# Attention scores from rounded halves of queries and keys, and one program block for the gate table and the experts

## The reference, cut to what matters

```
scores = einsum("brqhd,brkwhd->bhrqkw", q, k_g) * (dh ** -0.5) + bias   # local, 8 heads of 64, window 8 x 16
sc = einsum("bqngd,bknd->bngqk", qblk, k) * scale                       # group: 8 query heads, 2 key heads
sc = einsum("thpc,hpnc->thpn", q, sub_keys); top_s, top_i = top_k(sc, 16)
act = einsum("cd,ced->ce", xc, u[ic]); hid = gelu(act) * gc             # 128 experts per token
out = einsum("ce,ced->cd", hid, v[ic])
```

## Time and profile before

| what | value |
|---|---|
| median of 3 runs | 2273.9 us (2271.93 to 2278.22) |
| the profiled execution, its own time | 2281.19 us |
| its span, first to last instruction | 2278.3 us |
| busy: PE, DVE, ACT, POOL | 2155.6, 1501.3, 824.6, 671.5 us |
| mean granted TensorE clock | 0.973 of 2.4 GHz |
| phase_attend | about 128 to 244 us of the span |
| last product of phase_table, first of phase_experts | 1014.4 and 1027.4 us |

### The profile page before, as it was taken

How to read it: one execution, slowest core, us unless ns; L and a number is a source line. 1 busy time by engine, 2 the same in 40 slices (tenths; PEclk the granted TensorE clock), 3 DMA queues, 4 the chain that set the end, 5 groups by cost and what they waited for, 6 DMA issues and landing times. The chain is left out here.

```text
span 2278.3 us, 28638 instructions
## 1 busy us (share of the span) xinstructions
PE 2155.6 (95%) x10851; PEld 1863.2 (82%) x10851; DVE 1501.3 (66%) x2670; ACT 824.6 (36%) x1319; POOL 671.5 (29%) x440
## 2 busy tenths in 40 slices
PE   7999999999999999979999999999998999988899
PEld 6777788788999999979787877899986798876667
DVE  4645434425987889855889879869997534447644
ACT  3345423322333347733333333333334332222312
POOL 0100000000278877511434435436651000014200
PEclk9999999999999999999999999999998999988999
DMA  5321533301677878888999999979993222210320
GB/s 214 117 88 47 203 148 111 126 32 58 168 174 201 217 196 216 254 279 294 386 388 383 386 384 374 388 266 374 372 327 117 105 93 93 93 56 1 115 98 37
DMA packets 220232, 454.52 MB, mean 199 GB/s; under 512 B 32320, under 2 KB 137792, under 8 KB 213440
## 3 DMA queue, kind: packets, MB, share of 16 engines
q1 hardware_dynamic: 164800, 318.39, 40.9%
q0 software_dynamic: 55296, 134.31, 17.8%
HBM read 406.17 MB, written 46.47 MB: 199 GB/s over the span
## 5 line engine op out<-in xcount | busy, mean ns | idle before, releaser
L984 PE MATMUL bank<-XH,H 128*128 128x384 f32 x1024 | 349.8, 342 | 22.3 <-PEq L1229 12.6
L986 PE MATMUL bank<-XH,L 128*128 128x384 f32 x1024 | 345.8, 338 | 0.0
L985 PE MATMUL bank<-XL,H 128*128 128x384 f32 x1024 | 345.7, 338 | 0.0
L1734 PE MATMUL bank<-Vh,Hh 128*128 128x512 f32 x768 | 302.3, 394 | 17.0 <-DVE Hl L1829 17.0
L1735 PE MATMUL bank<-Vl,Hh 128*128 128x512 f32 x768 | 301.6, 393 | 0.0
L1736 PE MATMUL bank<-Vh,Hl 128*128 128x512 f32 x768 | 301.3, 392 | 0.0
L1065 POOL DMA_INDIRECT gates<-rows_sb x128 | 245.7, 1920 | 116.6 <-DVE rows_sb L1467 61.3
L1770 ACT ACTIVATE Vh<-Vr 128x1024 fp32r<-128x1024 f32 x128 | 135.8, 1061 | 293.4 <-PE bank L1736 151.8
L1021 POOL DMA_INDIRECT ring<-in_v,kq x128 | 186.3, 1456 | 177.5 <-DVE x_res L1033 76.3
L984 PEld LDWEIGHTS bank<-XH,H 128*128 128x128 f32 x1024 | 195.2, 191 | 26.0 <-issue 15.0
L985 PEld LDWEIGHTS bank<-XL,H 128*128 128x128 f32 x1024 | 195.0, 190 | 1.1
(11 more groups left out here) (393 smaller groups left out, 4398.3 us busy)
## 6 DMA issues: line engine op xcount, KB each, us to landing
Vr<-in_v SPq DMA_DIRECT2D x128, 512.0 KB
ur<-in_u SPq DMA_DIRECT2D x86, 512.0 KB
W<-in_w_stream SPq DMA_DIRECT2D x19, 2048.0 KB, 8.0
Gr<-gates SPq DMA_DIRECT2D x32, 768.0 KB
XT<-in_u SPq DMA_DIRECT2D x42, 512.0 KB
early<-ar SPq DMA_DIRECT2D x92, 192.0 KB
A<-early SPq DMA_DIRECT2D x92, 192.0 KB
XT<-in_w_mixer SPq DMA_DIRECT2D x14, 1024.0 KB
```

The costliest lines, as they stand in the source:

```text
L984: pe.matmul(ps, h[:, k], c.Xh[:, k, 0:DN], start=k == 0, stop=False)
L985: pe.matmul(ps, h[:, k], c.Xl[:, k, 0:DN], start=False, stop=False)
L986: mm = pe.matmul(ps, l[:, k], c.Xh[:, k, 0:DN], start=False, stop=k == KT - 1)
L1734: pe.matmul(ps, Hh[r][:, tok], Vh[r][:, cut], start=p == 0, stop=False)
```

## The change

Three things are changed together. (1) Scores: local attention uses halves of queries and keys, three fp32r products of 64 rows each (head h lies on partitions 0 to 63 or 64 to 127, with no padding). Group attention writes each query twice, on both halves of the partitions, and stacks the key's high half on its own 64 partitions and the low half on the other 64: one product of 128 rows gives hi x (hi + lo), a second one of 64 rows lo x hi. (2) The halves are made in phase_project: each group head is turned by PE, rounded by ACT and subtracted by DVE, in three portions of 4, 4 and 2 heads behind three pieces of projection; the memsets of `qz` go. Half of the storage is a slot of the weight ring, so one load of 2 MB (block 6) moves from phase_project to the end of phase_attend. (3) phase_table and phase_experts share one block. Loads of v and gates are written between the last eight turns of the table, the 14 dots are spread over the nine last conversions, six dots of the experts stand in the six lead blocks, PE waits for the table's copies before it reuses their banks.

```
@@ phase_project @@
+        def local_hi(act, g):
+            to, scale = (a.kh, 1.0) if g < 16 else (a.qh, DH ** -0.5)
+            act.activation(col_rows(to[:, g % 4]), by_col(bank(g)[:]), ACT.Copy, scale=scale).then_inc(grp_a, 1)
...
+        def turned_lo(dve, h):
+            dve.wait_ge(rout, h + 1)
+            if h < HEADS:
+                cut = own(h // 4)
+                dve.scalar_tensor_tensor(out=a.qgl[cut, h % 4], in0=c.bank[h % 4][cut, :], scalar=DH ** -0.5, in1=a.qgh[cut, h].bitcast(F32),
+                                         op0=ALU.mult, op1=ALU.subtract).then_inc(rout_d, 1)
...
+                if b != B_KA:
+                    c.load_w(sp, b + RING)
...
-            pool.memset(a.qz[:], 0.0).then_inc(set0, 1)
...
+                dve.tensor_tensor(a.q_rows[:, tt], twice(S1, ATT_W), twice(S2, ATT_W), ALU.add)
...
+                if 0 <= i - TURN < len(TURNED):
+                    for h in range(4 * (i - TURN), 4 * (i - TURN) + TURNED[i - TURN]):
@@ phase_attend @@
+            sp.wait_ge(scored, UNITS)
+            c.load_w(sp, B_KA + RING)
...
                     if h < HEADS:
-                        qT, kT = a.qz[:, h], a.kT[:, h // 2, KEY0[q]:KEY0[q] + KEYS]
+                        pe.matmul(ps, a.qh[cut, n, tok], a.kh[cut, n, keys], start=True, stop=False)
+                        pe.matmul(ps, a.qh[cut, n, tok], a.kl[cut, n, keys], start=False, stop=False)
+                        mm = pe.matmul(ps, a.ql[cut, n, tok], a.kh[cut, n, keys], start=False, stop=True)
                     else:
-                        qT, kT = a.qzb[:, h - HEADS], a.kTb[:]
-                    pe.matmul(psS[i % 3][:, 0:width(i)], qT[:, q * P:(q + 1) * P], kT, start=True, stop=True).then_inc(scored, 1)
+                        pe.matmul(ps, a.qgh[:, h - HEADS, tok], a.kg[:, n], start=True, stop=False)
+                        mm = pe.matmul(ps, a.qgl[cut, g, tok], a.kg[cut, n], start=False, stop=True)
+                    mm.then_inc(scored, 1)
@@ phase_table, phase_experts @@
-            turns(EL, E_LAST)
...
+            pe.wait_ge(copied, 2 * (DT - SCATTERED) * NSL)
...
-            fill(DOTS_TABLE, EARLY + 2)
+            los = count["lo"]
+            for n in range(los, EARLY + 2):
+                fill(DOTS_TABLE - D_LAST + D_LAST * (n + 1 - los) // (EARLY + 2 - los), n + 1)
...
-        block = ctx.enter_context(nc.Block())
...
+            for i in range(E_LAST):
+                early.turn(sp, EARLY - E_LAST + i)
+                if i == FREE:
+                    early.table_done(sp)
+                if FREE <= i < FREE + RR:
+                    load_v(i - FREE)
+                elif i == FREE + RR:
+                    sca.done(sp)
+                    load_g(0)
             for m in range(LEAD):
                 load_u(m + 3)
-                if m < RR:
-                    load_v(m)
...
             for q in range(LEAD):
                 lo_u(q + 2)
+                gat.dot(dve, DOTS_TABLE + q)
@@ build @@
+                block = joint.enter_context(nc.Block())
```

More of the change, by code:

```diff
@@ L194, in shared @@
         top = self.nc.sbuf_base
+        self.kq_at = top - (LOW + 4 * KT * P) * 4
         self.H, self.L = ([self.nc.alloc_sbuf_tensor_at(f"{n}{i}", [P, KT * P], F32R, offset=top - (at - i) * KT * P * 4)[:] for i in range(2)]
@@ L401, in out @@
             def out(b):
-                for g in range(4 * b, 4 * b + 4, 2 if b in (B_QB, B_KVB, B_QA) else 1):
+                for g in range(4 * b, 4 * b + 4, 2 if b in (B_QB, B_KVB) else 1):
                     act.wait_ge(grp, g + 1)
[L404 to L408, removed]
+                    if g < 12:
+                        project_out(g, copy, grp_a)
+                    else:
+                        if g == 12:
+                            act.wait_ge(roped, 1)
+                        if g == 16:
+                            act.wait_ge(rturn, HEADS + KV_HEADS)
+                        local_hi(act, g)
             for tt in range(0, TT, 2):
@@ L422, in _ @@
                     out(ends[i - 3])
[L423 to L428, removed]
+                if 0 <= i - TURN - 3 < len(TURNED):
+                    at = i - TURN - 3
+                    for h in range(4 * at, 4 * at + TURNED[at]):
+                        turned_hi(act, h)
             out(B_QA)
@@ L506, in _ @@
             link(last)
-            dve.wait_ge(set0, 2)
             for tt in range(TT):
[L509 to L514, removed]
+                twice = lambda x, w: x[:, tt, 0:w].rearrange("p (h w) -> p h w", w=DH).unsqueeze(2).broadcast_to([P, w // DH, 2, DH])
+                dve.tensor_tensor(a.q_rows[:, tt], twice(S1, ATT_W), twice(S2, ATT_W), ALU.add)
+                keys = lambda x: x[:, tt, ATT_W:].rearrange("p (h w) -> p h w", w=DH).unsqueeze(2).broadcast_to([P, KV_HEADS, 2, DH])
+                last = dve.tensor_tensor(KR[:, tt], keys(S1), keys(S2), ALU.add)
                 if tt == 1:
@@ L517, in _ @@
             last.then_inc(roped, 1)
-            for i in range(28, TURN + 4):
+            for i in range(28, N):
                 lo(i)
[L520 to L525, removed]
+                if i == TURN + 1:
+                    for g in range(12, 16):
+                        local_lo(dve, g)
+                if 0 <= i - TURN - 3 < len(TURNED):
+                    at = i - TURN - 3
+                    for h in range(4 * at, 4 * at + TURNED[at]):
+                        turned_lo(dve, h)
+            for g in range(16, 20):
+                local_lo(dve, g)
         @block.tensor
@@ L1210, in _, with phase_table @@
                                                  op0=ALU.mult, op1=ALU.mult).then_inc(gat.rows, 1)
-def phase_table(c, ijg, early, SC, gat, sca):
+def phase_table(c, ijg, early, SC, gat, sca, block):
     nc, t = c.nc, c.t
@@ L1619, in _, with phase_experts @@
             slices(2, EH[2])
-            fill(DOTS_TABLE, EARLY + 2)
-def phase_experts(c, early, gat, sca):
+            los = count["lo"]
+            for n in range(los, EARLY + 2):
+                fill(DOTS_TABLE - D_LAST + D_LAST * (n + 1 - los) // (EARLY + 2 - los), n + 1)
+def phase_experts(c, early, gat, sca, block):
     nc, t = c.nc, c.t
@@ L1781, in _ @@
                 if q == 1:
-                    early.table_done(act)
                     hi_v(0)
@@ L1840, in _ @@
             lo_h(0)
-            s, done = DOTS_TABLE, 0
+            s, done = DOTS_TABLE + LEAD, 0
             for p in range(PK):
@@ L2679, in inputs @@
     def inputs(self, c, ctx):
-        sb = lambda name, shape: ctx.enter_context(c.nc.sbuf_tensor(name, shape, F32))
-        self.qz = sb("qz", [P, HEADS, SEQ])
+        half = lambda name, n, at: c.nc.alloc_sbuf_tensor_at(name, [P, n, SEQ], F32R, offset=at)[:]
+        pairs = HEADS // 2
+        block = pairs * SEQ * 4
+        qz = ctx.enter_context(c.nc.sbuf_tensor("qz", [P, TT * ATT_W * 2], F32))
+        at = c.nc.sbuf_base - 2 * block
+        self.q_rows = qz[:].rearrange("p (t h c w) -> p t h c w", t=TT, c=2, w=DH)
+        self.qh, self.ql = half("qh", pairs, at), half("ql", pairs, at + block)
         self.kq = c.kq
-        self.kT = self.kq[:, 0:HEADS // 2 * SEQ].rearrange("p (h s) -> p h s", s=SEQ)
-        self.qzb = self.kq[:, HEADS // 2 * SEQ:].rearrange("p (h s) -> p h s", s=SEQ)
+        own = c.W_at + B_KA % RING * WBLK * 4
+        self.kh, self.qgh = half("kh", pairs, c.kq_at), half("qgh", HEADS, c.kq_at + block)
+        self.qgl, self.kl = half("qgl", pairs, own), half("kl", pairs, own + block)
+        self.kg = ctx.enter_context(c.nc.sbuf_tensor("kg", [P, KV_HEADS, SEQ], F32R))
         self.va = c.ur[:].rearrange("p r (a w) -> p (r a) w", w=ATT_W)
-        self.kTb = c.ar[:, 0]
         self.vb = c.ar[:, 1].rearrange("p (t w) -> p t w", t=TT)
@@ L2715, in build @@
                     phase_query(c, SC, early, gat, ask)
+                block = joint.enter_context(nc.Block())
                 if upto >= 5:
-                    phase_table(c, ijg, early, SC, gat, sca)
-            if upto >= 6:
-                phase_experts(c, early, gat, sca)
+                    phase_table(c, ijg, early, SC, gat, sca, block)
+            with joint:
+                if upto >= 6:
+                    phase_experts(c, early, gat, sca, block)
         with ExitStack() as mix:
```

65 lines of the change are left out of this document (36 added, 29 removed).

## The result

The changed kernel takes **2351.34 us** (median of 4 runs, 2345.08 to 2354.56) against 2276.06 us for the kernel before in the same comparison (4 runs): a ratio of 1.0315, 95% interval 1.0291 to 1.034. It is slower by some 75 us, where 13 us less were forecast. Its profiled execution took 2345.08 us and spans 2343.3; before it was 2281.19 and 2278.3.

What follows compares the result with a forecast made beforehand. PE was taken as the bound, busy 2155.6 of 2278.3 us. Gains of 12.8 (seam) + 1.6 (group) - 0.6 (local) - 0.4 (head turn) = 13.4 us gave 2273.9 - 13.4 = 2260.5 us, range 2245 to 2270.

Steps and rivals of the forecast that it cites:

- The sum: Whole kernel: seam 12.8 + group scores 1.6 - local scores 0.6 - extra head turn 0.4 = 13.4 us gained.
- rival four: Local attention: clock falls to 1.2 GHz; with half its units so, 2283 us; chance 0.05.
- 0.46 + 0.40: Group score: two products plus both row-count switches, 0.86 us against 0.91; 1.6 us gained over 32 units.
- rival one: Attention scores: switches cheaper than taken; free gives 2245.0 us (chance 0.07), only the drain paid 2250.5 (0.10).
- form (b): Attention scores: only the 0.09 drain is paid, the weight load hidden; 0.18 for both switches, 2250.5 us; chance 0.10.
- 2.80 us a pair: Local attention: PE's own sum of 1.40 a unit sets the pair, against 2.76 before; 0.6 us lost.
- Rival three: Local attention: the whole 0.27 us a unit is exposed, pairs near 3.3 us, time 2268.5; chance 0.12.
- 1.6 - 0.6 = 1.0: Attention: 1.6 us gained on group scores, 0.6 us lost on local scores.
- the gap and the half clock behind it: Seam of phase_table and phase_experts: 12.63 us barrier wait and 18 slow products go, 15.3 us gained.
- The single stall charged: Seam: one wait of PE for a late converted block, 2.5 us, taken off the 15.3 us.
- 12.8 us: Seam of phase_table and phase_experts: net gain forecast from joining the two blocks.
- rival two: Seam: DMA at 382 GB/s gives back 7.9 us, so the seam gives 7.4, time 2265.9; chance 0.16.

Runs made afterwards that it cites:

- e3_all_128rows: e2_group_128rows with the three products of a local score on all 128 rows too (that result left wrong): 2252.31 us, one run.
- e9_first3_128rows: Changed kernel with the second products of only the first three group scores on 128 rows: 2270.22 us, ratio 0.9964 to the kernel before.
- e10_first3_64rows: Changed kernel with second products on 64 rows only in the first three group scores, 128 in the other 29 units: 2262.21 us, one run.
- e1_joined_only: Kernel before with only the joined block of table and experts, attention unchanged: 2271.93 us against 2278.99, ratio 0.9974.
- e2_group_128rows: Changed kernel with the second product of every group score on 128 rows, local units unchanged: 2262.32 us, ratio 0.9924 to the kernel before.
- e6_burst: Changed kernel with six plain fp32 products on 128 rows added ahead of the first local unit: 2330.28 us, one run.
- e7_tiny_64rows: e2_group_128rows with a third product of 16 columns on 64 rows added to each group score: 2352.89 us, one run.

## Why the prediction was wrong

**The step that failed** is the clock. The sum priced every product of the attention at full clock, and the fall was rival four, at 0.05, for the local part and half of its units, 2283 us. Its argument against was that "a drained PE still has its products in the same time". This looked at columns and at busy time. Neither tells the kernels apart: `e3_all_128rows` streams as few columns for a score and keeps full clock, and the changed kernel sits at 1.2 GHz with PE busy for 50.00 of 50 us. Its place was wrong too. The clock falls at the first three group scores behind the gap between the phases. And its price was wrong, since it had no reason why a clock once lost would stay lost: with a product on 64 rows, and so a pair of changes of row count, in every unit it stays down for 198 us. `e9_first3_128rows` shows it from one side and `e10_first3_64rows` from the other. Price: 81 us, not 22. Why TensorE is granted less under such changes no run shows.

**Group scores.** Forecast 0.86 us a score, "0.46 + 0.40". At full clock it is 0.83, and a unit is 2.13 to 2.14, within the 2.1 to 2.2 forecast. The parts compensate, which is luck: two products on 128 rows are 0.54 and not 0.46, the two changes 0.29 and not 0.40. Units near 1.75 or 1.95, the signs of rival one, did not come, so neither of its forms gives the time. But the price of two changes, 0.29, lies halfway between the 0.18 of its form (b) and the 0.40 of the sum.

**Local scores.** Forecast 2.80 us a pair, 0.6 us lost in all. At full clock a pair takes 2.82, here in `e9_first3_128rows`:

```profile
226.39 0.38 PE L668 MATMUL bank<-kh,qh 64*128 64x256 f32 x1
...
227.70 0.38 PE L668 MATMUL bank<-kh,qh 64*128 64x256 f32 x1
...
229.21 0.38 PE L668 MATMUL bank<-kh,qh 64*128 64x256 f32 x1
```

From the first local score to phase_merge it is 50.2 us against 48.6, so the loss is 1.6, of which 0.6 come in the first three units, where the two kinds of attention overlap. The pair came out near the forecast, though not as it was worked out: PE's own sum is 1.31 a unit and not 1.40, and every second unit still waits for ACT's copy. Rival three (3.3 us a pair) is refuted.

**The rest of the attention.** At full clock, in `e9_first3_128rows`, the whole stretch from the first score to phase_merge takes 115.8 us against 116.6. That is 0.8 less, where 1.6 - 0.6 = 1.0 was forecast. Here too two misses compensate: the group part gains 2.4 us (with its first three scores on 128 rows), the local part loses 1.6. Block 6 of the weights arrived in time, and the conversions in the projection cost nothing: PE's gap ahead of the first product of phase_merge is 0.86 us, and the first score comes at 128.22 us against 128.0.

**The seam.** In the changed kernel the gap and the half clock behind it went as forecast. But of the twelve profiles with the joined block ten keep one stretch of 3.4 us at 1.2 GHz there (in `e1_joined_only` from 1031.9 us), of the 13.7 before the change. The single stall charged was 2.5 us; four waits of 6.8 us in all came, while ACT waited for blocks of u from DMA. So 12.8 us was too much, and 7 to 10 are there: rival two in part, whose 7.4 lies in the interval of `e1_joined_only`. That rival reckoned with 382 GB/s; the changed kernel moved 396 in the window shown.

With the clock held, as in `e9_first3_128rows`, the change would have given about 2270.2 against 2278.4 us in the same comparison, 8.2 less (3.9 to 12.3), where 13.4 were forecast. So the sum was some 5 us too high, the greater part of it at the seam, and its condition, full clock, was not met.

`e2_group_128rows` beats both kernels, by 16.7 us and 89 us. Of its gain over `e1_joined_only`, 9.6 us, its shorter attention explains 8.0 (108.6 against 116.6 us).

## What to carry to other kernels

A product on 64 rows between products on 128 costs 0.29 us of PE a pair of changes, which a sum can carry; it can also cost the clock, which a sum per product never shows. Where such changes recur in every unit, look at the granted clock at the entry of the phase: behind a gap, begin with units that have none, or use all 128 rows throughout where the extra rows do no harm to the result. And read the clock row of a profile before its busy row, since at 1.2 GHz PE looks perfectly used.

## What the runs showed of the hardware that I had not expected

- Two speeds of the same code. A pair of local units takes 4.60 us in the changed kernel and 2.82 in `e2_group_128rows`, `e6_burst` and `e9_first3_128rows`, at 1.2 and 2.4 GHz. Each level held to the end of the stretch, the low one for 198 us.
- A product of 16 columns on 64 rows, once a unit, was enough for the low state (`e7_tiny_64rows`).
- Plain fp32 products on 128 rows or group units without a change of row count raise the clock within a few microseconds (`e10_first3_64rows`, `e6_burst`).
- Getting into 64 rows costs 0.09 us and getting out 0.20, in fp32r products of 512 columns.
- Both kernels scatter by twice the gain at the seam: `e1_joined_only` from 2266.24 to 2280.7 us, the kernel before from 2272.79 to 2286.63. The spans of two single profiles, 2278.3 and 2264.4, promised 14 us where 12 and 17 runs gave 7.1.
